# Sixty-four experts' rows: from one memory slot per pair to two running sums that the scatters add into

## The chip, the cores and the metric

The kernel runs on one core of a Trainium2 chip. The metric is the device time of one execution in microseconds (us); lower is better. All numbers are float32, and the matrix products are done in three passes: each operand is split into a high part (rounded) and a low part (the rest), and high x high, low x high and high x low are added.

## The reference

512 tokens of width 1024 go through two blocks. The first is a hybrid layer (convolution and sparse attention) with a mixture of 64 experts behind it; the second has a latent-attention layer and a differential-attention layer, each with a gated feed-forward. Only the mixture matters here:

```
_, eidx = lax.top_k(scores + router_bias, 8)          # 8 experts of 64 for each token
g = take_along_axis(scores, eidx); g = g / sum(g) * 2.5
# every (token, expert) pair is one row: 512 * 8 = 4096 rows, sorted by expert
out    = swiglu(t[tok], w1[e], w3[e], w2[e]) * g      # 1024 -> 256 -> 1024
routed = segment_sum(out, tok, num_segments=512)      # each token's 8 rows are added
return routed + swiglu(t, ws1, ws3, ws2)              # x = x + gate2 * this
```

## The kernel before, in words

The activations live transposed in on-chip memory (X: 8 tiles of 128 features x 512 tokens). SyncE (SP) streams the weights in order through rings; ScalarE (ACT) makes the high part of each weight chunk of 128 x 1024 (`wh`, line 192), VectorE (DVE) the low part (`wl`, line 197), TensorE (PE) multiplies (lines 298 to 300).

**Setting up the experts** (about 380 to 445 us). Router scores, top 8 and gates are computed. Tokens' normalised rows and gates go to the memory tensor `h2rows` (512 x 1088 floats; lines 1580 and 1583 on SP). DVE makes each expert's list of pairs in rounds (`list_rounds`); `list_main` spreads the list into the tile LM (line 1706), which was zeroed at line 1766; PE transposes it, and `list_places` turns each code into two index columns per expert: `IDX`, the token number, and `YIX`, the pair number (token x 8 + rank, line 1739). An empty place gets a number out of bounds and its row moves nothing. Lists for rows past an expert's first 128 follow between the experts.

**The expert loop** (about 445 to 1060 us) is unrolled over the 64 experts, n = 0 to 63, in four programs that keep each other in step by semaphores. For each expert, weights come as three pairs of chunks (1 MB each, line 1974) into the ring `eraw` of 12 chunks, six pairs, and each load waits until DVE has split the pair that was in its place. On GpSimd's queue (POOL): `gate_column(n + 1)`, `gather(n + 4)` (line 2112, rows of `h2rows` by IDX into one of 4 slots of XG), then `scatter(n)`: it copies the expert's YIX column into a small tile (line 2121), waits for the result `YS` (ACT, line 2090, two slots) and for the copy, and sends the 128 x 1024 result to `expert_rows`, 4096 rows of 1024 floats, each to its pair's own row (line 2126). ACT writes a slot of YS again only when the scatter that reads it has landed (`y_out`).

**Experts with over 128 rows.** Extra blocks (`block_`, three in this input, about 1060 to 1098 us) do the same for the rest, one at a time, with their own gather and scatter (line 2435).

**The combination** (1098 to 1154 us). POOL signals `rows_whole` when all scatters have landed. SP then loads all of `expert_rows` back, 16 loads of 1 MB into 8 slots of YG (line 2397): four blocks of 128 tokens, each token's 8 rows of 1024 floats, two rows per load. For each block DVE adds two 128 x 2048 tiles (line 2540), adds the third and the fourth to them (line 2545, twice) and folds the halves (line 2547, YF). PE transposes YF in eight pieces (line 2561), and DVE adds each, times the gate, to X in 128 x 128 pieces (`back`, line 2530). Before the last block PE runs matmuls that nobody reads (`keep_clock(5)`, line 471).

**What follows.** The second block begins: three more `keep_clock` matmuls, a small product of `lamc` (lines 2579, 2580, 2587), the high parts of X (ACT, line 2594, 8 pieces) and the low parts (DVE, line 2600, 8 pieces), then the first products with weights whose first three chunks were split beforehand, at about 1096 to 1100 us.

Of the kernel before, what the change touches and what calls it, by code (L numbers as in the profile page):

```python
# [6 lines left out]
ALU = mybir.AluOpType  # L7
# [89 lines left out]
def build(nc, wstream, wada, cvec, consts, cols, rbias, positions, wexp, wrouter, lists, xT, out, first=True, second=True):  # L97
    with ExitStack() as ctx:
# [870 lines left out]
        if first:  # L969
# [581 lines left out]
            YIX = place("YIX", [P, 256], 10752, I32)  # L1551
# [15 lines left out]
            yrows = nc.dram_tensor("expert_rows", (S * 8, D), F32).ap()  # L1567
# [3 lines left out]
            def _(sp):  # L1571
# [160 lines left out]
            def list_places(dve, r):  # L1732

                dve.wait_ge(sem("list_t"), r + 1)
                if r == 0:
# [3 lines left out]
                nc.vector.tensor_scalar(YIX[:].rearrange("p (e r) -> p r e", r=4)[:, r, :], v, -1.0, EMPTY,  # L1739
                                        ALU.mult, ALU.add)  # L1740
# [8 lines left out]
            def _(dve):  # L1749
# [16 lines left out]
                nc.vector.memset(LM[:], 0.0)  # L1766
# [192 lines left out]
            YG = place("YG", [P, 16, D], 7168)  # L1959
            YA = place("YA", [P, 2, 2 * D], 0)  # L1960
            YF = place("YF", [P, 2, D], 4096)
# [23 lines left out]
            yix_at, gate_at = sem("yix_at"), sem("gate_at")  # L1985
# [143 lines left out]

            yg_in = [sem(f"yg_in{s}") for s in range(8)]  # L2130
            yg_used = sem("yg_used")
# [244 lines left out]
            def _(sp):  # L2376
# [31 lines left out]
            def _(pool):  # L2408
# [19 lines left out]
                def block_(p, i):  # L2428
                    y = 2 + p % 2
                    more_gate(p + 1, i)  # L2430
                    pool.tensor_copy(YIXC[:, y:y + 1], YIX[:, bass.ds(code_of(p, i), 1)])
# [3 lines left out]
                    pool.indirect_dma_start(out=yrows, out_offset=bass.IndirectOffsetOnAxis(ap=YIXC[:, y:y + 1], axis=0),  # L2435
                                            in_=YS[:, p % 2, :], in_offset=None,
                                            bounds_check=S * 8 - 1, oob_is_err=False).then_inc(ov["out"], 16)
# [84 lines left out]

            @stage("dve")
            def _(dve):
                def back(tb):
                    for half in range(2):
                        dve.wait_ge(sem("ya_t"), 2 * tb + half + 1)
                        for m in range(4):
                            x = X[:, 4 * half + m, tb * P:(tb + 1) * P]
                            last = nc.vector.scalar_tensor_tensor(  # L2530
                                out=x, in0=PS[:, 2 + half, m * P:(m + 1) * P],
                                scalar=cond[:, 40 + 4 * half + m:41 + 4 * half + m], in1=x, op0=ALU.mult, op1=ALU.add)
                        last.then_inc(sem("ya_read"), 1)
                def rows(n):
                    dve.wait_ge(yg_in[n % 8], 16 * (n // 8 + 1))
                    return YG[:, n % 8 * 2:n % 8 * 2 + 2, :].rearrange("p k d -> p (k d)")

                for tb in range(NB):
                    ya = YA[:, tb % 2, :]
                    nc.vector.tensor_tensor(ya, rows(4 * tb), rows(4 * tb + 1), ALU.add).then_inc(yg_used, 2)  # L2540
                    if tb:
                        back(tb - 1)
                    for n in (2, 3):
                        dve.drain()
                        nc.vector.tensor_tensor(ya, ya, rows(4 * tb + n), ALU.add).then_inc(yg_used, 1)
                    dve.drain()
                    nc.vector.tensor_tensor(YF[:, tb % 2, :], ya[:, 0:D], ya[:, D:2 * D], ALU.add).then_inc(sem("ya_whole"), 1)
# [642 lines left out]
```

## Time and profile before

| | |
|---|---|
| median of 3 runs | 2405.52 us (2403.63 to 2409.03) |
| the profiled execution | 2403.76 us, its span 2402.0 us |
| busy | PE 2260.3 us (94%), DVE 65%, ACT 50%, POOL 10% |
| memory traffic | 424.09 MB; mean 177 GB/s |
| combination, from the last scatter landed to the first product of the second block | 1098.2 to 1154.5 us |
| expert loop | about 9.33 us per expert |

Spans lie 1.8 us below the execution's own time. PE is the engine that the chain of waits runs through for 77% of the span; the combination is one of the places where it leaves PE. The trace also has the share of time in which the 16 DMA engines were busy and the GB/s that they moved.

### The profile page before, as it was taken

The page shows a single profiled execution, that of the slowest core. Times are in us where ns is not written, and L with a number is a line of the kernel's source. Part 1 is how long each engine was busy: PE and PEld are TensorE (multiplying, and loading weights), DVE is VectorE, ACT ScalarE, POOL GpSimd, SP SyncE. Part 2 cuts the span into 40 slices and gives each one's busy share as a digit, 9 for nine tenths or more (in the row PEclk, how much of TensorE's full clock was granted, in tenths as well). Part 3 has the DMA queues.
Part 4 walks back from the last instruction along what each step waited for, and adds up shares of the span by engine and source line. Part 5 has one row for each costly group of instructions (what it writes and reads, how often), then busy time and mean ns, then how long its engine had stood idle before and what let it go on. Part 6 is the DMA issues. An engine that isn't in the chain of part 4 may idle for free.

```text
span 2402.0 us, 30744 instructions
## 1 busy us (share of the span) xinstructions
PE 2260.3 (94%) x10236; PEld 1761.8 (73%) x10236; DVE 1568.2 (65%) x2403; ACT 1198.4 (50%) x1774; POOL 237.7 (10%) x312
## 2 busy tenths in 40 slices
PE   7999999899999999992999999999999889999997
PEld 5776676778888888872666788888778557888885
DVE  7789766899999999986665643333452676433344
ACT  4433434588888888871335332233222673322333
POOL 0000000333323333320000000000020000000000
PEclk9999999999999999996999999999999899999999
DMA  8411243799999999986220222223222001322332
GB/s 332 169 62 62 88 158 125 267 367 395 381 390 401 388 387 388 378 309 282 100 77 1 79 97 96 96 96 106 97 88 97 27 14 66 114 96 96 105 102 82
DMA packets 97377, 424.09 MB, mean 177 GB/s; under 512 B 20305, under 2 KB 20561, under 8 KB 70496
## 3 DMA queue, kind: packets, MB, share of 16 engines
q1 hardware_dynamic: 77168, 386.86, 43.6%
q0 software_dynamic: 19648, 34.72, 3.8%
q8 instruction: 72, 1.18, 0.2%
q10 hardware_dynamic: 432, 0.87, 0.1%
q14 instruction: 57, 0.47, 0.1%
HBM read 421.81 MB, written 39.45 MB: 192 GB/s over the span
## 4 chain that ended last, share of the span: by engine, by line
PE 77%; DVE 8%; issue 5%; ACT 5%; DMA 3%; DVEq 2%; SPq 0%; POOLq 0%; POOL 0%; ACTq 0%
PE PS L298 22%; PE PS L300 21%; PE PS L299 21%; ACT wh L192 3%; PE PS L714 2%; PE PS L2006 2%; PE PS L736 2%; DMA YG<-expert_rows 1%; DVE wl L197 1%; PE PS L725 1%; DMA ada_wa<-wada 1%; PE PS L2031 1%; DVEq L1285 1%; DVE M L1282 1%; PE PS L1245 1%
## 5 line engine op out<-in xcount | busy, mean ns | idle before, releaser
L197 DVE TENSOR_TENSOR wl<-raw,wh 128x1024 fp32r<-128x1024 f32 x239 | 292.4, 1225 | 357.1 <-ACT wh L192 350.9
L298 PE MATMUL PS<-HTh,wh 128*128 128x512 f32 x1248 | 498.5, 399 | 6.3 <-ACT V L881 2.2
L300 PE MATMUL PS<-HTh,wl 128*128 128x512 f32 x1248 | 486.9, 390 | 0.0
L299 PE MATMUL PS<-HTl,wh 128*128 128x512 f32 x1248 | 486.9, 390 | 0.0
L197 DVE TENSOR_TENSOR wl<-eraw,wh 128x1024 fp32r<-128x1024 f32 x384 | 458.5, 1221 | 17.5 <-ACT wh L192 14.5
L192 ACT ACTIVATE wh<-raw 128x1024 fp32r<-128x1024 f32 x239 | 252.0, 1056 | 368.9 <-PE PS L300 344.5
L192 ACT ACTIVATE wh<-eraw 128x1024 fp32r<-128x1024 f32 x384 | 392.5, 1054 | 16.8 <-PE PS L300 14.7
L298 PEld LDWEIGHTS PS<-HTh,wh 128*128 128x128 f32 x1248 | 234.5, 188 | 72.3 <-issue 13.7
L299 PEld LDWEIGHTS PS<-HTl,wh 128*128 128x128 f32 x1248 | 234.7, 188 | 50.0 <-issue 3.4
L300 PEld LDWEIGHTS PS<-HTh,wl 128*128 128x128 f32 x1248 | 234.7, 188 | 49.6
L298 PE MATMUL PS<-wh,XTh 128*128 128x512 f32 x536 | 221.1, 413 | 2.7 <-DVE wl L2192 1.5
L300 PE MATMUL PS<-wh,XTl 128*128 128x512 f32 x536 | 210.3, 392 | 0.0
L299 PE MATMUL PS<-wl,XTh 128*128 128x512 f32 x536 | 209.2, 390 | 0.0
L298 PE MATMUL PS<-AFh,wh 128*128 128x512 f32 x352 | 138.6, 394 | 0.0
L300 PE MATMUL PS<-AFh,wl 128*128 128x512 f32 x352 | 137.0, 389 | 0.0
L299 PE MATMUL PS<-AFl,wh 128*128 128x512 f32 x352 | 137.0, 389 | 0.0
L947 ACT ACTIVATE AFh<-AFf 128x512 f32 (+1 forms) x44 | 27.8, 632 | 182.4 <-DVEq L957 182.4
L298 PEld LDWEIGHTS PS<-wh,XTh 128*128 128x128 f32 x536 | 100.8, 188 | 22.1 <-DVE wl L2192 2.7
L300 PEld LDWEIGHTS PS<-wh,XTl 128*128 128x128 f32 x536 | 100.6, 188 | 22.2
L2126 POOL DMA_INDIRECT expert_rows<-YS,YIXC x64 | 76.7, 1199 | 387.2 <-ACT YS L2090 236.9
L299 PEld LDWEIGHTS PS<-wl,XTh 128*128 128x128 f32 x536 | 101.2, 189 | 16.9
L298 PE MATMUL PS<-wh,HHh 128*128 128x512 f32 x268 | 105.1, 392 | 4.5 <-DVE HHl L2511 2.8
(416 smaller groups left out, 3432.2 us busy)
## 6 DMA issues: line engine op xcount, KB each, us to landing
eraw<-wstream SPq DMA_DIRECT2D x192, 1024.0 KB, 7.5
raw<-wstream SPq DMA_DIRECT2D x240, 512.0 KB, 3.3
YG<-expert_rows SPq DMA_DIRECT2D x16, 1024.0 KB, 15.8
ada_w<-wada SPq DMA_DIRECT2D x20, 512.0 KB, 5.6
eraw<-wexp SPq DMA_DIRECT2D x9, 1024.0 KB, 6.8
ada_wb<-wada SPq DMA_DIRECT2D x2, 2048.0 KB, 15.5
ada_l<-wada SPq DMA_DIRECT2D x8, 512.0 KB, 3.4
ada_g<-wada SPq DMA_DIRECT2D x2, 2048.0 KB, 10.4
```

What stands on the lines that cost most here:

```text
L192: nc.scalar.activation(wh[:, ci % RING, :], src, ACT.Copy).then_inc(split_high, 1)
L197: nc.vector.tensor_tensor(wl[:, ci % RING, :], src, wh[:, ci % RING, :].bitcast(F32), ALU.subtract).then_inc(split_done, 1)
L298: nc.tensor.matmul(o, lh, rh, start=start, stop=False)
L299: nc.tensor.matmul(o, lh, rl, start=False, stop=False)
L300: return nc.tensor.matmul(o, ll, rh, start=False, stop=stop)
L714: mm = nc.tensor.matmul(PS[:, sbank(u, m), 0:P * (j + 1)], q[:, j * P:(j + 1) * P], k[:, 0:P * (j + 1)], start=x == 0, stop=x == len(prods ...
L725: mm = nc.tensor.transpose(PS[:, 4 + u % 2, kb * P:(kb + 1) * P], E_[:, u % 3, 0, kb * P:(kb + 1) * P], const("ident"))
L736: mm = nc.tensor.matmul(o, values(h, kb), Pt[:, u % 2, kb * P:(kb + 1) * P], start=kb == 0, stop=kb == j)
L947: nc.scalar.activation(ah(n, i), a_[:, n % 2, :], ACT.Copy).then_inc(s_h, 1)
L1245: nc.tensor.matmul(PS[:, 5 + n % 3, 0:P * (j + 1)], QI[b:b + HD, t, j * P:(j + 1) * P], KI[b:b + HD, 0:P * (j + 1)], start=True, stop=True ...
L2006: mm = nc.tensor.transpose(PS[:, 2 + m // 4, (m % 4) * P:(m % 4) * P + P], XG[:, n % 4, m * P:(m + 1) * P], const("ident"))
L2126: pool.indirect_dma_start(out=yrows, out_offset=bass.IndirectOffsetOnAxis(ap=YIXC[:, s:s + 1], axis=0), in_=YS[:, s, :], in_offset=None, b ...
```

## The change

`expert_rows` and `YIX` are gone. In their place are two sums in memory, `expert_sum0` and `expert_sum1`, of 512 x 1024 floats each, indexed by token. SP fills both with zeros from the zeroed tile LM (eight transfers of 512 KB, whose source is the same 128 floats repeated eight times); `list_main` waits until they have landed, since it overwrites LM. Each expert's scatter now adds its rows to the sum of its parity: the DMA engines read the destination row, add, and write it. It uses the IDX column in place, without the copy. Within an expert a token occurs once, and a scatter waits until the one before it on the same sum has landed. The extra blocks add to `expert_sum0`.

The combination loads the two sums in quarters of 256 columns (8 loads of 512 KB, 128 partitions x 4 blocks x 256 floats), adds them in one 128 x 1024 operation per quarter, transposes, and adds to X in pieces of 128 x 512. High and low parts of X are made in between.

```diff
-            yrows = nc.dram_tensor("expert_rows", (S * 8, D), F32).ap()
+            ysum = [nc.dram_tensor(f"expert_sum{s}", (S, D), F32).ap() for s in range(2)]
...
+                sp.wait_ge(sem("lm_zero"), 1)
+                for tb in range(NB):
+                    for s in range(2):
+                        sp.dma_start(ysum[s].rearrange("(b p) (c e) -> b p c e", p=P, e=P)[tb],
+                                     LM[:].unsqueeze(1).broadcast_to([P, DT, P])).then_inc(sem("sum_zero"), 16)
...
             def list_main(dve):
 
+                dve.wait_ge(sem("sum_zero"), 32 * NB)
...
-                nc.vector.tensor_scalar(YIX[:].rearrange("p (e r) -> p r e", r=4)[:, r, :], v, -1.0, EMPTY,
-                                        ALU.mult, ALU.add)
...
-                nc.vector.memset(LM[:], 0.0)
+                nc.vector.memset(LM[:], 0.0).then_inc(sem("lm_zero"), 1)
...
             def scatter(pool, n, i):
                 s = n % 2
                 if n >= 2:
-                    pool.wait_ge(y_out[s], i * 32 + 16 * (n // 2))
+                    pool.wait_ge(y_out[s], 16 * (n // 2))
                     pool.sem_inc(passed_pool, 1)
-                pool.tensor_copy(YIXC[:, s:s + 1], YIX[:, bass.ds(i * 16 + 4 * n, 1)]).then_inc(yix_at, 1)
+                elif n == 0:
+                    pool.wait_ge(sem("sum_zero"), 32 * NB)
+                    pool.sem_inc(passed_pool, 1)
                 pool.wait_ge(y_ready, i * 4 + n + 1)
                 pool.sem_inc(passed_pool, 1)
-                pool.wait_ge(yix_at, i * 4 + n + 1)
-                pool.sem_inc(passed_pool, 1)
-                pool.indirect_dma_start(out=yrows, out_offset=bass.IndirectOffsetOnAxis(ap=YIXC[:, s:s + 1], axis=0),
-                                        in_=YS[:, s, :], in_offset=None,
-                                        bounds_check=S * 8 - 1, oob_is_err=False).then_inc(y_out[s], 16)
+                pool.indirect_dma_start(out=ysum[s], out_offset=bass.IndirectOffsetOnAxis(ap=IDX[:, 4 * n:4 * n + 1], axis=0),
+                                        in_=YS[:, s, :], in_offset=None, bounds_check=S - 1, oob_is_err=False,
+                                        compute_op=ALU.add).then_inc(y_out[s], 16)
...
-                for n in range(NB * 4):
-                    if n >= 8:
-                        sp.wait_ge(yg_used, n - 7)
-                    sp.dma_start(YG[:, n % 8 * 2:n % 8 * 2 + 2, :].rearrange("p k d -> p (k d)"),
-                                 yrows.rearrange("(b p k) d -> b p (k d)", p=P, k=8)[n // 4][:, n % 4 * 2 * D:(n % 4 + 1) * 2 * D]
-                                 ).then_inc(yg_in[n % 8], 16)
+                for q in range(4):
+                    for s in range(2):
+                        sp.dma_start(YF[:, s, q, :, :], ysum[s].rearrange("(b p) (q d) -> q p b d", p=P, q=4)[q]
+                                     ).then_inc(ya_in[q], 16)
...
+                def back(m):
+                    dve.wait_ge(sem("ya_t"), m + 1)
+                    nc.vector.scalar_tensor_tensor(out=Xm(m), in0=PS[:, SUM_BANK[m % 4], :], scalar=cond[:, 40 + m:41 + m],
+                                                   in1=Xm(m), op0=ALU.mult, op1=ALU.add).then_inc(sem("ya_read"), 1)
...
+                for q in range(4):
+                    dve.wait_ge(ya_in[q], 32)
+                    nc.vector.tensor_tensor(YF[:, 0, q, :, :], YF[:, 0, q, :, :], YF[:, 1, q, :, :], ALU.add).then_inc(sem("ya_whole"), 1)
+                    if second and q:
+                        x2_low(2 * q - 2)
+                        x2_low(2 * q - 1)
+                    back(2 * q)
+                    back(2 * q + 1)
+                if second:
+                    x2_low(DT - 2)
+                    x2_low(DT - 1)
...
             def _(pe):
+                pe.wait_ge(sem("rows_whole"), 1)
+                keep_clock(3)
+                for m in range(DT):
+                    if m % 2 == 0:
+                        pe.wait_ge(sem("ya_whole"), m // 2 + 1)
+                    if m >= 4:
+                        pe.wait_ge(sem("ya_read"), m - 3)
+                    for tb in range(NB):
+                        mm = nc.tensor.transpose(PS[:, SUM_BANK[m % 4], tb * P:(tb + 1) * P],
+                                                 YF[:, 0, m // 2, tb, m % 2 * P:(m % 2 + 1) * P], const("ident"))
+                    mm.then_inc(sem("ya_t"), 1)
```

Both `keep_clock` places of before (ahead of the last block, and ahead of the product of `lamc`) are gone; one of three matmuls now stands behind `rows_whole`.

DVE's program at the combination: before, for the first block and the next (YA, YG: tiles of 2048 columns; X in 128 x 128 pieces).

```order
L2540 TENSOR_TENSOR YA<-YG 128x2048 [waits yg_in1,yg_in0]
L2545 TENSOR_TENSOR YA<-YA,YG 128x2048 [waits yg_in2]
L2545 TENSOR_TENSOR YA<-YA,YG 128x2048 [waits yg_in3]
L2547 TENSOR_TENSOR YF<-YA 128x1024
L2540 TENSOR_TENSOR YA<-YG 128x2048 [waits yg_in5,yg_in4]
L2530 SCALAR_TENSOR_TENSOR X<-PS,cond,X 128x128 [waits ya_t]
L2530 SCALAR_TENSOR_TENSOR X<-PS,cond,X 128x128 x3
L2530 SCALAR_TENSOR_TENSOR X<-PS,cond,X 128x128 [waits ya_t]
L2530 SCALAR_TENSOR_TENSOR X<-PS,cond,X 128x128 x3
```

DVE's program at the same place in the changed kernel, whole.

```order
L2541 TENSOR_TENSOR YF<-YF 128x1024 [waits ya_in0]
L2527 SCALAR_TENSOR_TENSOR X<-PS,cond,X 128x512 [waits ya_t] x2
L2541 TENSOR_TENSOR YF<-YF 128x1024 [waits ya_in1]
L2532 TENSOR_TENSOR HTl<-X,HTh 128x512 [waits x2h] x2
L2527 SCALAR_TENSOR_TENSOR X<-PS,cond,X 128x512 [waits ya_t] x2
L2541 TENSOR_TENSOR YF<-YF 128x1024 [waits ya_in2]
L2532 TENSOR_TENSOR HTl<-X,HTh 128x512 [waits x2h] x2
L2527 SCALAR_TENSOR_TENSOR X<-PS,cond,X 128x512 [waits ya_t] x2
L2541 TENSOR_TENSOR YF<-YF 128x1024 [waits ya_in3]
L2532 TENSOR_TENSOR HTl<-X,HTh 128x512 [waits x2h] x2
L2527 SCALAR_TENSOR_TENSOR X<-PS,cond,X 128x512 [waits ya_t] x2
L2532 TENSOR_TENSOR HTl<-X,HTh 128x512 [waits x2h] x2
```

The sixteen wide operations on whole rows became four, and six of the eight low parts (HTl) moved ahead of the last pieces of X.

POOL's program in the expert loop: before, one expert.

```order
L2099 COPY GS<-XG 128x1 [waits xg_in0,hid_full]
L2112 DMA XG<-h2rows,IDX 128x1088 [waits xg_in3,xt_ps,gate_at]
L2121 COPY YIXC<-YIX 128x1 [waits y_out1]
L2126 DMA expert_rows<-YS,YIXC 4096x1024 [waits y_ready,yix_at]
```

POOL's program for the same expert in the changed kernel.

```order
L2100 COPY GS<-XG 128x1 [waits xg_in0,hid_full]
L2113 DMA XG<-h2rows,IDX 128x1088 [waits xg_in3,xt_ps,gate_at]
L2127 DMA expert_sum<-YS,IDX 512x1024 [waits y_out1,y_ready]
```

The wait for the earlier scatter on the same parity moved from the copy to the scatter itself; the number of scatters and the rows in each are the same.

## Rows read from the trace of the kernel before

**Rows 1.** The chain in order of time, combination: start us, us, what.
```profile
1094.92 3.31 DMA expert_rows<-YS,YIXC
1098.40 2.55 issue
...
1103.58 14.68 DMA YG<-expert_rows
...
1121.07 18.41 DMA YG<-expert_rows
...
1144.02 6.73 PE PS L471 x10
```

**Rows 2.** Timeline, combination: start us, us, engine, line, operation [idle before it].
```profile
1101.02 26.84 SPq L2397 DMA_DIRECT2D YG<-expert_rows  x16
1108.47 2.29 DVE L2540 TENSOR_TENSOR YA<-YG 128x2048 f32<-128x2048 f32 x1 [7.92 <-DMA YG<-expert_rows]
...
1115.69 1.23 DVE L2547 TENSOR_TENSOR YF<-YA 128x1024 f32<-128x1024 f32 x1
1116.98 1.97 PE L2561 MATMUL PS<-K,YF 128*128 128x128 f32 x8 [23.99 <-DVE YF L2547]
...
1150.58 1.04 PE L2561 MATMUL PS<-K,YF 128*128 128x128 f32 x8
...
1153.70 4.90 DVE L2600 TENSOR_TENSOR HTl<-X,HTh 128x512 fp32r<-128x512 f32 x8
...
1154.54 0.47 PE L298 MATMUL PS<-HTh,wh 128*128 128x512 f32 x1 [0.22 <-DVE HTl L2600]
```

**Rows 3.** Stretches: us, busy of PE, PEld, DVE, ACT, POOL, PEclk, DMA share, GB/s.
```profile
1117.00:1144.00 27.00, 5.88 (x24) 4.68 (x24) 24.61 (x33) 0.00 (x0) 0.00 (x0) 0.50 1.01 420
1144.00:1148.00 4.00, 3.98 (x5) 1.85 (x6) 3.85 (x2) 0.00 (x0) 0.00 (x0) 0.50 0.56 224
1148.00:1151.00 3.00, 3.00 (x10) 1.31 (x9) 1.95 (x2) 0.00 (x0) 0.00 (x0) 0.93 0.00 0
```

**Rows 4.** Stretches, expert loop, two of five of 90 us.
```profile
560.00:650.00 90.00, 89.22 (x440) 73.24 (x439) 86.61 (x97) 79.59 (x96) 29.37 (x40) 1.00 1.00 389
...
830.00:920.00 90.00, 89.71 (x439) 73.83 (x438) 86.93 (x96) 80.51 (x97) 28.24 (x38) 1.00 1.00 393
```

**Rows 5.** Stretches, a single expert of the loop.
```profile
768.00:777.30 9.30, 9.30 (x48) 7.76 (x47) 8.85 (x10) 8.39 (x11) 2.60 (x4) 1.00 1.02 425
```

**Rows 6.** DMA view, 560 to 1010 us: packets; queue: packets, MB, share of 16 engines.
```profile
DMA packets 34183, 174.81 MB, mean 388 GB/s; under 512 B 10022, under 2 KB 10022, under 8 KB 15891
...
q0 software_dynamic: 13606, 24.80, 14.3%
```

**Rows 7.** Tile eraw, 470 to 1060 us: from issue to landing.
```profile
DMA to landing us min/median/max: 5.0/7.6/10.9
```

**Rows 8.** Tile YS, 470 to 1060 us: from issue to landing.
```profile
DMA to landing us min/median/max: 3.5/8.1/10.5
```

**Rows 9.** Timeline, ACT and POOL over one expert.
```profile
606.68 1.03 ACT L2090 ACTIVATE YS<-PS 128x1024 f32<-128x1024 f32 x1 [0.24 <-PE PS L300]
...
608.69 1.02 POOL L2126 DMA_INDIRECT expert_rows<-YS,YIXC  x1 [6.56 <-ACT YS L2090]
...
616.04 1.03 ACT L2090 ACTIVATE YS<-PS 128x1024 f32<-128x1024 f32 x1 [0.26 <-PE PS L300]
```

**Rows 10.** Stretch, setting up the experts.
```profile
400.00:412.00 12.00, 11.83 (x71) 9.71 (x71) 10.80 (x30) 3.94 (x8) 3.55 (x8) 1.00 0.00 0
```

**Rows 11.** Timeline, DVE and SP, setting up the experts.
```profile
391.60 0.17 DVE L1766 MEMSET LM<- 128x128 f32 x1
...
412.69 0.89 SPq L1580 DMA_DIRECT2D h2rows<-G  x2
...
430.96 0.32 DVE L1706 COPY LM<-LL 64x64 f32<-64x64 f32 x2
...
432.38 0.75 DVE L1887 SCALAR_TENSOR_TENSOR X<-PS,cond,X 128x512 f32<-128x512 f32 x1
```

More of the change, by code:

```diff
@@ L1550, in build @@
             IDX = place("IDX", [P, 256], 10496, I32)
-            YIX = place("YIX", [P, 256], 10752, I32)
             IDXC = place("IDXC", [P, 8], 11008, I32)
@@ L1958, in build @@
             YS = nc.alloc_sbuf_tensor_at("YS", [P, 2, D], F32, offset=HT_AT)
-            YG = place("YG", [P, 16, D], 7168)
-            YA = place("YA", [P, 2, 2 * D], 0)
-            YF = place("YF", [P, 2, D], 4096)
+            YF = place("YF", [P, 2, 4, NB, 256], 3072)
             @stage("sp")
@@ L2434, in block_ @@
                     pool.sem_inc(passed_pool, 1)
-                    pool.indirect_dma_start(out=yrows, out_offset=bass.IndirectOffsetOnAxis(ap=YIXC[:, y:y + 1], axis=0),
-                                            in_=YS[:, p % 2, :], in_offset=None,
-                                            bounds_check=S * 8 - 1, oob_is_err=False).then_inc(ov["out"], 16)
+                    pool.indirect_dma_start(out=ysum[0], out_offset=bass.IndirectOffsetOnAxis(ap=YIXC[:, y:y + 1], axis=0),
+                                            in_=YS[:, p % 2, :], in_offset=None, bounds_check=S - 1, oob_is_err=False,
+                                            compute_op=ALU.add).then_inc(ov["out"], 16)
                     pool.wait_ge(ov["rows"], i * (16 * GROUP) + 16 * (p + 3))
@@ L2520, in _ @@
                     split_dve(dve, EXPERT1 + c)
+            SUM_BANK = (2, 3, 6, 7)
             @stage("dve")
             def _(dve):
[L2525 to L2547, printed above, removed]
@@ L2548, in _, with x2_low @@
-                back(NB - 1)
+                def back(m):
+                    dve.wait_ge(sem("ya_t"), m + 1)
+                    nc.vector.scalar_tensor_tensor(out=Xm(m), in0=PS[:, SUM_BANK[m % 4], :], scalar=cond[:, 40 + m:41 + m],
+                                                   in1=Xm(m), op0=ALU.mult, op1=ALU.add).then_inc(sem("ya_read"), 1)
+                def x2_low(m):
+                    dve.wait_ge(sem("x2h"), m + 1)
+                    nc.vector.tensor_tensor(Hl(m), Xm(m), Hh(m).bitcast(F32), ALU.subtract).then_inc(sem("x2l"), 1)
@@ new lines, in _ @@
+                if second:
+                    for t in range(2):
+                        nc.vector.tensor_tensor(lamc[:, t:t + 1], col("lam", 2 * t), col("lam", 2 * t + 1), ALU.mult)
+                    nc.vector.tensor_scalar(lamc[:, 5:6], col("g_sub"), 1.0 - LAMBDA_INIT, None, ALU.mult)
+                    dve.drain().then_inc(sem("lam_p"), 1)
+                for q in range(4):
[6 more added lines that the diff above has]
+                    back(2 * q + 1)
@@ L2550, in _ @@
+                if second:
+                    x2_low(DT - 2)
+                    x2_low(DT - 1)
             @stage("pe")
             def _(pe):
-                for tb in range(NB):
-                    if tb == NB - 1:
-                        pe.wait_ge(sem("ya_read"), 2 * tb)
-                        keep_clock(5)
-                    pe.wait_ge(sem("ya_whole"), tb + 1)
-                    for half in range(2):
-                        if tb:
-                            pe.wait_ge(sem("ya_read"), 2 * (tb - 1) + half + 1)
-                        for m in range(4):
-                            mm = nc.tensor.transpose(PS[:, 2 + half, m * P:(m + 1) * P],
-                                                     YF[:, tb % 2, (4 * half + m) * P:(4 * half + m + 1) * P], const("ident"))
-                        mm.then_inc(sem("ya_t"), 1)
+                pe.wait_ge(sem("rows_whole"), 1)
@@ L2574, in build @@
             VM = place("VM", [P, NB, 2, 512], 18432)
-            @stage("dve")
-            def _(dve):
-                for t in range(2):
-                    nc.vector.tensor_tensor(lamc[:, t:t + 1], col("lam", 2 * t), col("lam", 2 * t + 1), ALU.mult)
-                nc.vector.tensor_scalar(lamc[:, 5:6], col("g_sub"), 1.0 - LAMBDA_INIT, None, ALU.mult)
-                dve.drain().then_inc(sem("lam_p"), 1)
             @stage("pe")
             def _(pe):
-                keep_clock(3)
                 pe.wait_ge(sem("lam_p"), 1)
@@ L2592, in _ @@
                     if first:
-                        act.wait_ge(sem("ya_read"), 2 * NB - 1 + m // 4)
+                        act.wait_ge(sem("ya_read"), m + 1)
                     nc.scalar.activation(Hh(m), Xm(m), ACT.Copy).then_inc(sem("x2h"), 1)
-            @stage("dve")
-            def _(dve):
-                for m in range(DT):
-                    dve.wait_ge(sem("x2h"), m + 1)
-                    nc.vector.tensor_tensor(Hl(m), Xm(m), Hh(m).bitcast(F32), ALU.subtract).then_inc(sem("x2l"), 1)
             RKV = place("RKV", [P, S], 22528)
```

7 lines of the change are left out of this document (3 added, 4 removed).

## The prediction

> **What bounds the kernel now.** I read the chain of waits first, in order of time, around the change: it says what the end of the kernel hangs on at each moment. In the combination it runs through the DMA engines: the last scatter lands, 2.55 us pass until SP issues, and then two long pieces of 14.68 and 18.41 us are waits for YG loads, followed by 6.73 us of PE's unread matmuls [rows 1]. The timeline gives the frame: the first load is issued at 1101.02, PE's first useful product of the second block starts at 1154.54 [rows 2]. The stretches say why it is long: 420 GB/s at a DMA share of 1.01, while PE is busy 5.88 of 27 us [rows 3]. 16 MB have to come back through engines that move 420 to 425 GB/s at best [rows 3, 5]. DVE is nearly as busy as the transfers there, so it has to shrink too, and it does.
>
> Then the expert loop, since the change touches each of its scatters. PE is busy 89.2 to 89.7 us of 90 at full clock: PE sets the pace, 9.33 us per expert (from one YS to the next in [rows 9] it is 9.36). But the DMA engines are at a share of 1.00 and move 389 to 393 GB/s [rows 4], while a single expert shows 425 [rows 5]. So PE is the bound with some 8% of room in the transfers behind it. The weights' loads land 7.6 us after their issue, 10.9 at most [rows 7], and a place of the ring is needed again six pairs, 18.7 us, after it was refilled, so nothing waits for them today. This room is where the prediction is decided.
>
> **The combination, step by step.** (1) The last scatter lands 3.31 us after its issue [rows 1]. Now each row must also be read in memory first. No row of before shows an adding scatter: the price lies between 0 more (the read runs beside the other) and once more the whole, 3.3. I take 0.7, near the low end, because the scatters in the loop land from 3.5 us on although the weights pass beside them [rows 8]. Issue of the first load: 1101.7. (2) Before, 2.1 MB (two loads) were there 7.45 us after the first issue [rows 2]; at 420 GB/s [rows 3] 5.0 of these are transfer and 2.45 are start and end. A quarter is two loads of 0.52 MB: 2.45 + 2.5. Its pieces are 1 KB long instead of 8 KB; nothing in these rows prices that, the bounds are 0 and as much again (2.5); I take 0.5, by the neighbouring 4 KB rows that pass in the loop at 425 GB/s. First quarter there: 1107.1. (3) From there DVE sets the pace: one addition of 128x1024 (1.23 us), two low parts (4.90 / 8 = 0.61 each) [rows 2] and two pieces of 128x512 out of the matmul banks (0.75 each) [rows 11] make 3.95 us a quarter, longer than the 2.5 to 3.0 us in which a quarter lands, so the transfers hide behind DVE after the first. The first quarter has no low parts but waits for transposes: 1.23 + 0.9 + 1.5 = 3.6. Two quarters more: 7.9. The addition of the fourth: 1.23. Eight transposes: 1.04 at full clock, 1.97 at half [rows 2], I take 1.5; the small product: 0.4. Together 14.6 us: PE starts at 1121.7 instead of 1154.5, that is 32.8 us earlier. The last two low parts come behind, but PE then works through six tiles that are ready, 4 us.
>
> (4) The clock. PE stood at 0.50 through the old combination, and only 4 us of unread matmuls brought it to full before the last block [rows 3]. Now three unread matmuls come about when the loads are issued, and then transposes with pauses between them. If PE enters the second block at half clock, the first 4 us of products run at half speed and 2 us are lost; if not, 0. I take 1. Combination: **31.8 us less**, between 24 and 34.
>
> **Zeroing the sums.** 4.2 MB of writes can start after the memset at 391.60 and are waited for by the list at 430.96 [rows 11]. In between, from 400 to 412, the engines stood at 0.00 [rows 10]. At 420 GB/s they take 10 us; at half that rate 20, which would end about when SP has to send the gates at 412.69 [rows 11]. SP's eight issues take no more than 0.45 us each (the two of that row took 0.89). Cost 0; the cover is 39 us for the list and 21 for the queue of `h2rows`. If it were gone, each us would delay the first gather.
>
> **The loop.** Removed: a copy on POOL per expert and four short DVE operations; POOL stands idle 6.56 us before each scatter [rows 9], so the copy was free: 0. Unchanged: a scatter waits for the one two experts before, issued 18.7 us earlier and landed after at most 10.5 [rows 8]: 0. An issue on POOL takes 1.02 us [rows 9] and may take 6 times as long before anything is late.
>
> The transfers: POOL's queue moved 24.80 MB in 450 us, 55 GB/s [rows 6], gathers of 1088 floats and scatters of 1024 in equal number; scatters are 27 of it. Reading each destination row adds a second read of the same size. Charged like a plain row, the load is 388 + 27 = 415 GB/s, against the 425 that one expert reached [rows 5]: it fits, with 2% of room. Bounds: 0 (it all fits) and, if no more than the 393 already seen over a long stretch [rows 4] can be held, 415 / 393 = 5.6% of 590 us, 33 us. I take **4 us more**, close to the low end, because rows 5 is a full expert at the higher rate while the ring's slack evens out single experts.
>
> This price per row can be set against the Trainium skill: its page "Collectives: The Full Stack" (section "The bandwidth ceiling: the fold count and why AG ≠ RS ≠ AR") says that an add in the DMA path costs nothing by itself, but needs two source reads in one engine's queue, which halves the rate. No run here shows it yet. By that rule a row costs two plain rows, and the sum stays as it is; if an adding row cost only what the plain one of this trace does, the loop would add 0 and the kernel take 2374.
>
> The three extra blocks wait for their scatter one after the other, but PE's own work of a block is longer; 0 to 2 us, in the range.
>
> **Sum.** -31.8 + 4 = -27.8 against the profiled execution, 2403.76: 2376. The median of the three runs is 1.76 higher, 2405.52, so I forecast **2378 us**.
>
> **Rivals.** (A) The room in the loop is smaller than one expert's 425 suggests: at a true ceiling of 402, halfway down to the long means, 415 costs 3.2%, 19 us, and the kernel takes about 2393. For: a share of 1.00 at 389 GB/s says that the engines are never seen idle [rows 4]. Against: landing times stay at 7.6 us where 17 would do [rows 7]. (B) The adding scatter is far dearer than two plain rows, for instance because an engine waits for the memory's answer between read and write. The place is the loop. The gain of 31.8 us is 5.4% of 590 us, so the break-even is a demand of 448 GB/s, 60 more than now: **a row at 3.2 plain rows**. The same would show if a scatter landed later than 16.6 us: a YS slot is written again 18.7 us later, and the scatter starts 2 us after the write began [rows 9]. At five plain rows: (388 + 108) / 425 = 1.17, 98 us more, 2472: slower. For: no row prices it, and the DMA share is 1.00. Against: 16.6 us leave double today's median landing, 8.1. (C) The quarters' 1 KB pieces pass at half rate: a quarter per 5 us, the last at about 1124, PE at 1127: 5.5 us of the gain are lost, 2383. That is inside my forecast's range. That the change does not do what it says I exclude: 4 MB instead of 16 are loaded, whatever the order.
>
> **How the numbers follow.** About 0.2% (4.8 us) is what a measurement of this kernel tells from no change. My forecast with its bounds (2368 to 2389, rival C in it): 0.60. Rival A (2389 to 2400.7): 0.15. A loop that eats just the gain (within 0.2%): 0.05. Rival B (above 2410): 0.18. Better than 2368: 0.02. So faster 0.77, same 0.05, slower 0.18. The range from 2368 to 2404 leaves out rival B and the last sliver.
>
> **What would show it.** In the changed profile: from the first load's issue to PE's first product about 20 us instead of 53.5; the first addition some 5.4 us after the issue, then one about each 4 us with DVE never waiting for a load; in the loop 9.33 to 9.4 us per expert, no waits on eraw, weight loads landing somewhat later than 7.6 us, scatters near 9. I am wrong if the experts' period exceeds 9.5 us, if ACT waits for a scatter before YS, if the zeros land after 412 us, or if additions wait for quarters.

## The result and the profile after

The changed kernel takes **2375.60 us** (median of 4 runs, 2374.59 to 2377.54) where the kernel before took 2404.57 (4 runs) beside it: a ratio of 0.9889, 95% interval 0.9871 to 0.9906. Measured again on another occasion (last experiment) the ratio was 0.9915, 0.9901 to 0.9930. About 1% faster, by both. The forecast was 2378, range 2368 to 2404.

The chain of the changed kernel in the combination (start us, us, what) answers to [rows 1]:

```profile
1076.00 6.34 DMA expert_sum<-YS,YIXC
...
1099.97 5.05 DMA expert_sum<-YS,YIXC
...
1105.19 2.82 issue
...
1108.08 0.37 SPq L2396
...
1108.50 6.77 DMA YF<-expert_sum
1115.30 1.24 DVE YF L2541
...
1116.58 1.98 PE PS L2561 x8
...
1118.59 0.75 DVE X L2527
1119.34 1.15 DVE YF L2541
```

The two waits of 14.68 and 18.41 us for YG have become one of 6.77 for YF. After it the chain alternates between DVE and PE and meets no transfer. The last scatter takes 5.05 us to land where it took 3.31. The timeline of PE (columns as in [rows 2]):

```profile
1108.11 4.66 PE L471 MATMUL PS<-K 128*128 128x512 f32 x6 [10.05 <-POOLq L2445]
1116.58 1.97 PE L2561 MATMUL PS<-K,YF 128*128 128x128 f32 x8 [3.81 <-DVE YF L2541]
1120.53 1.97 PE L2561 MATMUL PS<-K,YF 128*128 128x128 f32 x8 [1.98 <-DVE YF L2541]
...
1130.46 0.77 PE L298 MATMUL PS<-HTh,wh 128*128 128x512 f32 x1
```

From the first load's issue to the first product of the second block it is 22.4 us (1108.08 to 1130.46); before it was 53.52 (1101.02 to 1154.54).

The expert loop, as a stretch of 450 us and in the DMA view of the same stretch (columns as in [rows 3, 6]; then line, operation, number, KB each, median us from issue to landing):

```profile
560.00:1010.00 450.00, 447.95 (x2198) 368.61 (x2197) 433.54 (x481) 400.60 (x476) 180.57 (x144) 1.00 1.02 391
```

```profile
DMA packets 34395, 175.91 MB, mean 391 GB/s; under 512 B 10063, under 2 KB 10063, under 8 KB 16012
...
q1 hardware_dynamic: 20646, 150.34, 80.2%
q0 software_dynamic: 13717, 25.16, 21.8%
...
eraw<-wstream SPq DMA_DIRECT2D x143, 1024.0 KB, 10.5
expert_sum<-YS,IDX POOLq DMA_INDIRECT x48, 9.3
```

PE stays as busy as before (448 of 450 us). What changed is POOL's queue q0: nearly the same bytes as in [rows 6], 25.16 instead of 24.80 MB, but 21.8% of the engines' time instead of 14.3. The price of adding is there, and the loop's pace does not pay it. The shares need care: q1, the weights' queue, shows 80.2% here, while in the kernel with plain scatters below it shows 85.1% for the same bytes. The time of packets depends on what runs beside them, so only shares of kernels with equally full engines can be set against each other.

Four stretches hold the whole account. Their bounds are the first and the last YS of the 64 experts and the first LAT row of the second block (L898), all from the timelines; each difference is mine:

| us | start to first YS | first to last YS | last YS to LAT | LAT to the end |
|---|---|---|---|---|
| before | 462.3 | 595.5 | 107.3 | 1236.9 |
| after | 463.3 | 599.1 | 79.4 | 1233.9 |
| after, again | 462.6 | 598.7 | 77.7 | 1237.9 |

The change gives 28 to 30 us in the third stretch and takes 3 to 4 back in the loop. Cut at the 61st YS, the loop tells more (us, from the starts of YS in ACT's timelines; the last four kernels are explained below):

| kernel | first to 61st YS | 61st to last YS |
|---|---|---|
| before | 570.8 | 24.7 |
| after, both profiles | 569.1 | 30.0 and 29.6 |
| all scatters plain | 569.0 | 28.2 |
| plain double | 599.0 | 33.0 |
| adding double | 633.6 | 34.4 |
| adding for every other | 598.3 | 29.3 |

Over the first sixty experts the changed kernel is 1.7 us faster, with or without adding; what it is due to wasn't tried. Over the last three it loses 5.3 and 4.9 us. The 3 us of the first profile in the last stretch are not its own: the same kernel again had 1237.9, and the kernels below 1234 to 1241.

### The profile page after: what moved, and what is told of

It is laid out like the page before. It is cut to its first block, busy times and chain, and to the rows that moved or that the text cites. A ratio compares the mean times of both kernels' runs of the same rounds, so it can differ in the third digit from the quotient of the medians.

```text
span 2375.7 us, 30540 instructions
## 1 busy us (share of the span) xinstructions
PE 2256.5 (95%) x10226; PEld 1760.5 (74%) x10226; DVE 1536.6 (65%) x2363; ACT 1198.8 (50%) x1774; POOL 286.1 (12%) x248
## 4 chain that ended last, share of the span: by engine, by line
PE 77%; DVE 9%; issue 5%; ACT 4%; DMA 2%; DVEq 2%; POOLq 0%; SPq 0%; POOL 0%; ACTq 0%
PE PS L298 22%; PE PS L300 21%; PE PS L299 21%; PE PS L714 3%; DVE wl L197 2%; PE PS L2007 2%; ACT wh L192 2%; PE PS L736 2%; PE PS L725 1%; DMA ada_wa<-wada 1%; DMA expert_sum<-YS,YIXC 1%; PE PS L2032 1%; DVE XTl L2060 1%; PE PS L1245 1%; DVEq L1285 1%
## 5 line engine op out<-in xcount | busy, mean ns | idle before, releaser
L2127 POOL DMA_INDIRECT expert_sum<-YS,IDX x64 | 115.0, 1796 | 343.2 <-ACT YS L2091 211.3
L947 ACT ACTIVATE AFh<-AFf 128x512 f32 (+1 forms) x44 | 27.8, 632 | 182.4 <-DVEq L957 182.4
```

Of the source, the lines that this page charges most:

```text
L947: nc.scalar.activation(ah(n, i), a_[:, n % 2, :], ACT.Copy).then_inc(s_h, 1)
L2127: pool.indirect_dma_start(out=ysum[s], out_offset=bass.IndirectOffsetOnAxis(ap=IDX[:, 4 * n:4 * n + 1], axis=0), in_=YS[:, s, :], in_offse ...
```

## The experiments

My theory at this point: the gain is the combination; adding costs no pace in the loop, but 5 to 7 us at its end, in the three blocks and in the last landing; a row that is added costs two plain ones. The changed kernel itself came out 19 and 29 us below the one before on two occasions, so differences of a few us between the medians of these kernels tell nothing; I read the small effects from the traces, one for each kernel.

**All scatters plain, and the blocks' alone.**

```diff
-    in_=YS[:, s, :], ..., oob_is_err=False, compute_op=ALU.add)     # loop
+    in_=YS[:, s, :], ..., oob_is_err=False)
-    in_=YS[:, p % 2, :], ..., compute_op=ALU.add)                   # blocks
+    in_=YS[:, p % 2, :], ...)
```

> All scatters of experts and of the three blocks overwrite rows instead of adding to them; addresses, sizes, loads and waits are those of the changed kernel, so the output is not the sum. Theory (the add costs nothing in the loop and 5 to 7 us at its end): ACT's wait before the last expert's YS (4.6 us) goes, the blocks' scatters land in about 3.3 instead of 5 to 6.3 us, the last one lands 1.7 us sooner, the loop keeps 9.33 us per expert; 2368 to 2371, 5 to 7 us below the changed kernel. Rival (the add costs pace in the loop that the long stretches hide, as my forecast's 4 us had it): the middle of the loop itself gets shorter by 4 us or more, 2362 to 2366. Rival (the 4.5 us at the end of the loop come from POOL's order and not from the add): the wait before the last YS stays, 2373 to 2375.

> The 64 scatters of the loop add, the scatters of the three blocks overwrite. Theory: of the 5 to 7 us some 4.4 belong to the last loop scatters, and stay; the blocks' own waits and the last landing (1.7 us) give 2 to 2.5 us back: 2373 to 2374, with the first load's issue 2 to 2.5 us earlier than in the changed kernel. Rival (the blocks, which wait for one scatter after another, pay the most): 4 us or more back, 2371 or less.

Measured: 2374.05 (ratio 0.9879, 0.9857 to 0.9902) with all plain, 2373.62 (0.9879, 0.9858 to 0.9901) with only the blocks' plain. Against either measurement of the changed kernel this doesn't settle a difference. 2368 to 2371 was wrong, and what came is what the second rival said: 2373 to 2375, with the wait before the last YS still there (4.15 us, for PE). The stretches do tell. First to last YS: 597.2 all plain, 598.7 with the loop adding, as in the changed kernel. From the last YS to the issue of the first load: 42.9 and 43.6 us, against 45.7 and 45.4 in the two profiles of the changed kernel: adding in the blocks costs 2 us or a little more, as expected. But of the 5 us that the last three experts lose against before, 3.5 stay without any adding; only 1.4 to 1.8 are the add's. The plain kernel's DMA view, same stretch:

```profile
q1 hardware_dynamic: 20603, 150.05, 85.1%
q0 software_dynamic: 13680, 24.94, 14.4%
...
eraw<-wstream SPq DMA_DIRECT2D x143, 1024.0 KB, 7.8
expert_sum<-YS,IDX POOLq DMA_INDIRECT x48, 8.0
```

Share and landings of before are back, with the new addresses and sums: of the 7.5 points that q0's share rose against before, 7.4 are the add.

**A second scatter for each expert: plain, adding, and adding for every other expert of a slot.**

```diff
+    pool.indirect_dma_start(out=ydummy[s], ..., in_=YS[:, s, :], ...)   # e4: compute_op=ALU.add
-    act.wait_ge(y_out[s], i * 32 + 16 * (n // 2))
+    act.wait_ge(y_out[s], 32 * (n // 2))
```

> Behind each of the 64 adding scatters a second one writes the same rows to a memory that nobody reads, overwriting; a YS slot is free when both are through. It adds one plain row per row: 27 GB/s more. If an adding row costs two plain rows, the demand is 388 + 27 + 27 = 442 GB/s against the 425 that one expert showed: 4% or 24 us more in the loop, 2400, with PE waiting for weights in the loop. If an adding row costs about one plain row, the demand is 415 and the time stays within 4 us of 2376. If the ceiling lies well above 425, nothing changes either, and the adding double tells.

> The same with the second scatter adding too, into the memory that nobody reads. If an adding row costs two plain rows: 388 + 4 x 27 - 27 = 469 GB/s against 425, 10% or 61 us more in the loop, 2437, and 37 us more than with the plain double. If it costs one plain row: 415 GB/s, the same as the plain double. If it costs three (rival B of the prediction): 388 + 2 x 54 + 27 = 523, 23% or 136 us more, 2510.

> The second adding scatter behind every second expert of a slot alone, 32 instead of 64. In rows: 64 + 32 adding ones. If an adding row costs two plain rows, this asks of the DMA engines what the plain double asks (388 + 27 + 27 = 442 GB/s) and takes its time, 2413; if it costs one, half of what the plain double adds, 2394; if three, 2437. If not the rows but the number of scatters in the queue counts (64 extra ones took 37 us when plain), 32 extra ones take 19, 2395.

Measured: 2413.22 (2411.32 to 2418.32), 2453.70 (2453.30 to 2459.60) and 2404.94 (2399.94 to 2408.27): 37.6, 78.1 and 29.3 us over the changed kernel's first median. Their DMA views, 560 to 1010 us, plain double:

```profile
DMA packets 38785, 177.02 MB, mean 393 GB/s; under 512 B 13042, under 2 KB 13042, under 8 KB 21534
...
q0 software_dynamic: 19380, 35.55, 27.3%
```

adding double:

```profile
DMA packets 36192, 165.96 MB, mean 369 GB/s; under 512 B 11991, under 2 KB 11991, under 8 KB 20093
...
q0 software_dynamic: 18086, 33.93, 32.3%
```

every other one:

```profile
DMA packets 35445, 170.58 MB, mean 379 GB/s; under 512 B 11173, under 2 KB 11173, under 8 KB 18294
...
q0 software_dynamic: 16156, 29.93, 27.5%
```

*The price of a row.* Share times 450 us by the experts in the stretch (48 in the plain and the changed kernel, 45, 42 and 45 here) is q0's time per expert: 1.35 us all plain, 2.04 changed, 2.73 with a second plain scatter, 3.46 with a second adding one, 2.75 with half of one. So a plain scatter adds 0.69, an adding one 1.42, half of one 0.71: **an adding row takes 2.06 times a plain one**. These three differences are between kernels whose engines are equally full: q1's share per MB is 0.53 to 0.54% in all four. Against the plain kernel the comparison is rougher, since q1 has 0.57% per MB there: a gather row has 1088 floats and a scatter row 1024, so of the 1.35 us the plain scatter has 0.655, and adding raises it by 0.69, or by some 0.77 if q0's plain share is scaled as q1's (an estimate). The times say the same without any share: up to the 61st YS, sixty more plain scatters cost 29.9 us (599.0 against 569.1), sixty more adding ones 64.5, thirty more adding ones 29.2. Measured so, the price agrees with the rule of the Trainium skill ("Collectives: The Full Stack", section "The bandwidth ceiling: the fold count and why AG ≠ RS ≠ AR") that the prediction weighed (a second source read, half the rate).

*The ceiling.* A scatter moves 24.94 MB / 48 x 1024 / 2112 = 0.252 MB. Each adding scatter's read counted once more, the engines carry 391 + 27 = 418 GB/s in the changed kernel, 393 + 25 = 418, 369 + 47 = 416 and 379 + 37 = 416 in the three doubles. Four kernels, nearly one number, and PE is held up in the last three. **The changed kernel stands just below the ceiling.** From 418 to 445 and 472 of demand, over 417, would be 40 and 78 us in a loop of 595. The loops (first to last YS) took 33 and 69 us more (631.9 and 668.1 against 599.1), so I estimate 7 to 9 us of room, 1 to 1.5% of the loop, which agrees with the changed kernel's pace being untouched. The whole kernels took 38 and 78 us more, the rest lying outside the loop. The absolute forecasts (2400 and 2437) had 425 as the ceiling and were 13 and 17 us short; the difference between them, 37, was measured as 40.5.

The half double should by this take as long as the plain double, and up to the 61st YS it does: 598.3 and 599.0 us. That also answers the rival of that experiment by which the number of scatters counts and not the rows: 32 more scatters cost what 64 did. That it took 8 us less in all comes from the end: the last three experts took 29.3 against 33.0 us, and behind the last YS the plain double needs another 5.4 us more up to LAT (83.3 and 77.9), perhaps because its last expert has two scatters to land and this one's has one. Who waits differs too. PE and ACT, 560 to 1010 us (who, for what: us in all, times, longest), in the adding double:

```profile
PE PS L2008 <- DMA XG<-h2rows,IDX: 39.0, 24, 3.5
...
ACT YS L2092 <- DMA expert_dummy<-YS,IDX: 39.1, 26, 3.4
```

and with every other one:

```profile
ACT wh L192 <- DMA eraw<-wstream: 60.8, 79, 2.0
```

With two scatters behind every expert the gathers and the YS slots, both in q0, are late and the weights hardly (with the plain double 20.9, 19.5 and 2.7 us of waits); with one and a half it is the weights. Why the queues share the full engines in this way I didn't try.

**Issue and pieces of the loads.** The second sum's four loads moved to ACT's queue, and 4 KB rows instead of 1 KB pieces:

```diff
-    for s in range(2): sp.dma_start(YF[:, s, q, :, :], ysum[s]...[q])
+    sp.dma_start(YF[:, 0, q, :, :], ysum[0]...[q])       # e5; the same with 1 from ACT
-    ysum[s].rearrange("(b p) (q d) -> q p b d", p=P, q=4)[q]
+    ysum[s].rearrange("(b p) d -> b p d", p=P)[q]        # e8
```

> The four quarters of the second sum are loaded from ACT's queue, beside SP's four of the first. Theory (the first addition comes 7.2 instead of 5.4 us after the issue because SP takes 1.1 us for each issue and a quarter needs two): the second load of the first quarter is issued 1.1 us sooner, the first addition comes 6.1 us after the first issue, 1 to 1.3 us less in all, about 2374.5. Rival (the 1 KB pieces pass slowly, whoever issues them): the first addition stays at 7 us, 2375.5.

> The same eight loads of 512 KB, but as blocks of 128 rows of 4 KB instead of column quarters with 1 KB pieces, 128 descriptors instead of 512 each; what is added lies in another place than it should, so the output is not the reference's. Theory (descriptors cost, 1 KB pieces too): SP's issues take 0.45 instead of 1.1 us, the first addition comes 5.3 us after the first issue as forecast instead of 7.2, 1.9 us less, 2373.7. Rival (landing time of the load is the same): the issues get shorter, the first addition comes at 6.5 us, 0.7 us less.

Measured: 2375.24 (0.9880, 0.9857 to 0.9903) and 2373.50 (0.9868, 0.9842 to 0.9894), no difference that can be told. In the timelines the two queues issue their four loads in 2.4 and 2.7 us:

```profile
1104.52 2.37 SPq L2395 DMA_DIRECT2D YF<-expert_sum  x4
1104.52 2.74 ACTq L2500 DMA_DIRECT2D YF<-expert_sum  x4
1109.85 1.23 DVE L2545 TENSOR_TENSOR YF<-YF 128x1024 f32<-128x1024 f32 x1 [8.97 <-DMA YF<-expert_sum]
```

and long rows take 4.35 us for eight instead of 8.78:

```profile
1103.90 4.35 SPq L2396 DMA_DIRECT2D YF<-expert_sum  x8
1108.88 1.23 DVE L2541 TENSOR_TENSOR YF<-YF 128x1024 f32<-128x1024 f32 x1 [10.28 <-DMA YF<-expert_sum]
```

The first addition comes 5.33 and 4.98 us after the first issue, against 7.22 in the first profile of the changed kernel. But the kernels with unchanged loads spread from 4.90 (blocks plain) to 7.22, and the changed kernel again had 5.98. So the issues are shorter for sure; that this brings the first addition forward is likely, not shown.

**The clock.**

```diff
-    keep_clock(3)
+    keep_clock(6)
     for m in range(DT):
         if m % 2 == 0:
+            if m: keep_clock(1)
```

> Six unread matmuls instead of three ahead of the transposes, and one ahead of each further quarter. Theory (PE works at half clock through the combination: a transpose group takes 1.97 us, and the first products of the second block lose 0.7 us): at full clock a quarter's transposes take 1.04 us, the last quarter 0.9 us less, the first products nothing; 1.5 us less, 2374, and the granted clock of the stretch is 0.9 or more. Rival (DVE sets the pace and the unread matmuls delay the transposes): no gain or up to 2 us more.

Measured: 2375.94 (0.9874, 0.9847 to 0.9901). In the trace it does what it should (PE's timeline):

```profile
1111.98 1.09 PE L2563 MATMUL PS<-K,YF 128*128 128x128 f32 x8 [1.58 <-DVE YF L2541]
...
1115.27 1.09 PE L2563 MATMUL PS<-K,YF 128*128 128x128 f32 x8 [1.34 <-DVE YF L2541]
...
1123.65 0.48 PE L298 MATMUL PS<-HTh,wh 128*128 128x512 f32 x1
```

From the first addition to the first product it is 12.96 us instead of 15.16, a quarter takes 3.65 instead of 3.95, the first product 0.48 instead of 0.77. The granted clock of 13 us from the first transposes on, changed kernel and this one:

```profile
1117.00:1130.00 13.00, 7.07 (x32) 5.87 (x31) 11.94 (x16) 3.78 (x6) 0.00 (x0) 0.50 0.74 257
```

```profile
1111.00:1124.00 13.00, 7.28 (x42) 4.76 (x43) 12.25 (x17) 3.78 (x6) 0.00 (x0) 1.00 0.87 304
```

From the first addition to LAT some 3 us are won, and the last stretch of the same run is 1239.7 us: the median doesn't show them, nor the 2374 that was expected.

**The end of the loop.** First POOL's scatter ahead of its gather for the last four experts; then, since that lost, only the third but last scatter and the last expert's gates moved ahead of the last gather:

```diff
     elif n + 2 < E:                      # e7: scatter(pool, n, i) ahead of this for n >= E - 4
         more_gather(pool, p, ...)
-    scatter(pool, n, i)
+    if n == E - 3:                       # e9, ahead of more_gather
+        gate_column(pool, n + 2)
+        scatter(pool, n, i)
```

> For the last four experts POOL issues the scatter ahead of the gather for the blocks. Theory (the 4.5 us that the last expert loses come from the scatter of the third but last expert, issued late behind POOL's gather and then landing in 9 us): ACT's wait before the last YS goes, the last scatter of the loop is issued about 4.5 us earlier, 2371 to 2372. Rival (the blocks' own adding scatters, one after another, take the place): the first block's scatter comes no earlier than now, 2375.

> POOL fetches the last expert's gates and issues the scatter of the third but last expert ahead of its last gather for the blocks, where it stands 7.6 us; the first gather for the blocks keeps its place. Theory (the loop's end loses to POOL's order in two ways: the gates of the last expert come 2.7 us late, PE stops and its clock falls for some 4 us, and the YS slot comes free late): PE no longer waits for HG of the last expert, its clock stays at full, ACT does not wait for the scatter; last YS 4 us earlier against the first YS (599.1 us from the first YS to the last now, 594.5 to 595.5 then), about 2371.5. Rival (the later second gather holds up the first block's transposes, as the first gather did when the order was changed in the whole): what the loop gains comes back in the blocks, 2375.

> POOL's order as above and the seven more unread matmuls of the clock experiment. Theory: the two gains lie in different places and add: 4 us at the end of the loop, 3 us from the first addition to the first rows of the second block (transposes of a quarter 1.04 instead of 1.97 us, and no products at half clock), 2368.5. Rival: with a full clock earlier, the chip takes it back later in the second block, and the sum stays at 2371.

Measured: 2385.65 (0.9915, 0.9892 to 0.9938), some 10 us over its neighbours of the same chip; 2376.22 (0.9890, 0.9868 to 0.9911); 2375.32 (0.9890, 0.9870 to 0.9910). The first one lost since the first gather for the blocks moved from 1038.89 to 1043.37 (counted from the first YS, 6.8 us later), and PE waited for its rows and the gates (PE's timeline):

```profile
1045.21 0.69 PE L2032 MATMUL PS<-K,HG 128*128 128x128 f32 x2 [4.49 <-DVE HG L2072]
1050.87 1.42 PE L2163 MATMUL PS<-K,XG 128*128 128x128 f32 x8 [2.52 <-DMA XG<-h2rows,IDXC]
```

Its loop is 603.0 us long. The wait of the last YS for a scatter was indeed gone: I had moved the wrong instruction. What happens in the changed kernel is this (POOL, PE and ACT of its timeline):

```profile
1050.59 1.78 POOL L2153 DMA_INDIRECT XG<-h2rows,IDXC  x1 [6.88 <-issue]
...
1052.68 1.60 POOL L2127 DMA_INDIRECT expert_sum<-YS,IDX  x1 [0.31 <-issue]
...
1055.05 0.44 PE L2032 MATMUL PS<-K,HG 128*128 128x128 f32 x2 [2.74 <-DVE HG L2072]
...
1062.41 1.03 ACT L2091 ACTIVATE YS<-PS 128x1024 f32<-128x1024 f32 x1 [4.61 <-DMA expert_sum<-YS,IDX]
```

POOL stands 6.88 us before the gather (the trace names no releaser; 5.37 in the kernel before), the scatter and the last gates come after it, PE waits 2.74 us for HG where before it waited 0.89, and its granted clock is 0.72 in 1055 to 1060, where it was 1.00 before the change. Counted from the first YS, that product with HG comes only 0.7 us later than before (591.8 and 591.1); from it to the last YS it then takes 7.4 us (6.9 in the second profile) instead of 4.4. So most of the loss is in the stretch of lower clock and not in the wait itself. With the gates first (PE and ACT, the same two places):

```profile
1052.08 0.44 PE L2032 MATMUL PS<-K,HG 128*128 128x128 f32 x2 [0.72 <-DVE HG L2072]
...
1056.52 1.03 ACT L2091 ACTIVATE YS<-PS 128x1024 f32<-128x1024 f32 x1 [1.69 <-PE PS L300]
```

the loop is 594.2 us, 4.9 less, as expected, and from HG to the last YS it takes 4.4 us again; 1.8 come back behind it (81.2 instead of 79.4 from the last YS to LAT: the second block's gather is later). In the third kernel PE waited just as short a time (0.72), and yet the clock dipped at that place (0.70 in 1055 to 1060; 6.0 us from HG to the last YS) and the loop was 595.9: the pause alone does not settle the clock. From the first YS to LAT the last two need 675.5 and 674.7 us, the changed kernel 678.5 and 676.4. That is 1 to 4 us better in the traces and not to be told in the medians: the expected 2371.5 and 2368.5 were missed by 5 and 7 us. So there is no version here of which I can say that it beats the changed kernel.

**The changed kernel again.**

> The changed kernel once more, unedited, to see which of the small differences belong to it. From the first YS to the last, 599.1 us in its first profile: if the loss at the loop's end (POOL late, the clock's fall, the wait for the YS slot) is the change's own, 598 to 600 again, if it was chance 595.5 as before the change. From the last YS to the first rows of the second block, 79.4 us: the same within 1. From there to the end, 1233.9 us against 1236.9 before the change: if the 3 us belong to the change, 1234 again; if they are chance (the other runs lie between 1234 and 1241), anything in that range. Issue of the first load to the first addition: 7.2 us if that is the kernel's own, 4.9 to 7.2 if it varies as in the other runs.

Measured: 2381.16 (2378.67 to 2381.29; 0.9915, 0.9901 to 0.9930), on a chip on which the kernel before took 2400.10. The loop's end is the change's own (598.7), the last stretch is not, and the wait from issue to first addition varies (5.98). Here the last YS waited for PE and not for the scatter (PE's clock 0.50 in 1055 to 1060), and came only 0.4 us sooner after the first: the slot's wait of 4.61 us stands beside PE's own delay. That is also why the kernel with only the blocks plain, which shows no such wait, has the same 598.7.

## Why the prediction was right

The forecast gain against the profiled execution was 27.8 us, the profiled runs gave 26.2 (2403.76 to 2377.54), the medians 29 and 19. The mechanism held: four times less to load, a chain paced by DVE behind it, a loop still paced by PE. Part of the number is luck: 3 us of the first profile's 26.2 are the last stretch, which the second profile doesn't have, and the steps were off in both directions.

- **(1) The last scatter**, +0.7 us forecast: measured +1.74, and with the blocks' own waits for each other +2.5 up to the first issue (45.7 instead of 43.2 from the last YS). Inside the bounds of 0 to 3.3, but I had picked the low end from loop landings, which barely moved (8.2 to 9.3 us) because in the loop a plain scatter too takes 8 us, against 3.3 us for the last one behind the blocks [rows 1].
- **(2) The first quarter there** 5.4 us after the issue: 7.2 and 6.0. I had priced the issue at no more than a place in the queue; eight loads take SP 8.78 us, and a quarter needs two. The 0.5 us for short pieces went by the bytes and left the issue out. How much of the 1.8 us is the issue stays open: with only the blocks plain, the same loads were there after 4.90.
- **(3) DVE sets the pace** with 3.95 us a quarter: additions at 1115.30, 1119.26, 1123.20 and 1127.15, none waiting for a load. Exact. From the first addition to PE 15.2 us, forecast 14.6: the transposes ran wholly at half clock, 1.97 us.
- **(4) The clock**, 1 us: from the first product to LAT 11.4 (again: 11.8) instead of 10.5 us, so 0.9 to 1.3.
- **Combination**: 31.8 forecast, 27.9 and 29.6 measured from the last YS to LAT. Rival C, inside the range, did not come: no addition behind the first waited.
- **Zeroing**, cost 0: right, though by another margin. The eight issues took 10.58 us, not at most 0.45 each, and the gates' rows left SP at 413.67 instead of 412.69. The zeros were there in time: the last store was issued at 402.0, and none took more than 7.1 us to land:

```profile
392.83 10.58 SPq L1580 DMA_DIRECT2D expert_sum<-LM  x8
413.67 0.39 SPq L1584 DMA_DIRECT2D h2rows<-G  x1
```

- **The loop**, +4 us: +3.6 and +3.2, but for another reason. I had expected it spread over 590 us as the price of a nearly full DMA; the first sixty experts were 1.7 us faster instead, and 5 us are lost in the last three, where POOL comes late and the clock falls, 3.5 of them without any adding too. That the forecast and the measured loop agree is luck. The price of a row, two plain ones, was right; the room was smaller: some 1 to 1.5% below a ceiling of 416 to 418, where I had 415 against 425 [rows 5]. A single stretch of 9.3 us says what the engines can do for a moment, the doubles what they can hold. It cost nothing because PE's pace lies just below the ceiling, and landings of 10.5 us for the weights and 9.3 for the scatters still fit into 18.7.
- **Rival A** (a ceiling of 402) is refuted by 416 to 418, and by the pace of the loop. Its 402 was also not "halfway" between 425 and the long means of 389 to 393; that would be 408, 10 us instead of 19. **Rival B** needed 3.2 plain rows; it is 2.06. Of the right answer some was luck: the adding double shows how near the edge is, since 27 GB/s more cost 38 us (the plain double), more than the whole gain.

## What to carry to other kernels

An accumulating scatter that replaces a write, a read back and a sum is worth its doubled price per row where rows come back many at a time; count each adding row as two in the DMA budget, and compare with a rate that the engines have held over a long stretch, found by adding traffic until the time moves. Before reordering a helper engine's queue at the end of a pipelined loop, look for everything queued behind each slow instruction: moving the last experts' scatters ahead of the blocks' gathers lost 10 us, while moving one scatter and the last gates won 1 to 4 us in the traces, too little for the medians to show.

## What the runs showed of the hardware that I had not expected

- An adding indirect scatter costs POOL more to issue: 1.60 us against 1.02 [rows 9] for the same 128 rows; with all scatters plain in the changed kernel the median was 1.01 us, against 1.60.
- SP's issue of a 512 KB load takes 0.9 to 1.1 us with 1 KB pieces (7.47 and 8.78 us for 8 in the two profiles) and 0.54 with 4 KB rows (4.35 for 8); with the zero fill's eight stores it was 1.3 (10.58 for 8).
- Six unread matmuls in place of three, and one ahead of each quarter, kept the granted clock at 1.00 (2.4 GHz) over a stretch where PE was busy 7.3 of 13 us, while 7.1 of 13 us without them was granted 0.50 (1.2 GHz).
- At the loop's end pauses of PE of 1.9 to 2.7 us for HG went with a granted clock of 0.50 to 0.86 in the next 5 us. With a pause of 0.7 to 0.9 us it stayed at 1.00 in two kernels (the one before, and that with the gates first) and fell to 0.70 in a third. What decides there stays open.
